# The first pair of a Strassen-style feed-forward layer: the low part of T3 made before the sum T4, and B12 loaded before B21

## The chip, the cores and the metric

One core of one Trainium2 chip runs the whole program in one launch. The metric is the device time in microseconds (us), as the median of the runs of a kernel. Nothing is shared with another core.

## What is computed

Two transformer blocks on 256 tokens of width 1024, batch 1, all in float32. The first block has a forgetting attention beside a multi-scale pooling, an attention over 256 memory tokens, and a gated feed-forward layer. The second has two layers, each of them feed-forward, mixer (a short gated convolution in one, a differential attention in the other), feed-forward. That makes five feed-forward layers, and they are what matters here. Each is

```python
gu = xn @ w_gate_up                                # (256, 1024) @ (1024, 2 * 2816)
act = silu(gu[..., :2816]) * gu[..., 2816:]
h = h + act @ w_down                               # (256, 2816) @ (2816, 1024)
```

(in the second block, what is added is normed and halved first).

## The kernel before

**Precision.** Every float32 weight tile of 128 x 2048 is split into a high part (`w_hi`, made by ScalarE with a copy to the matmul's rounded format, L768 or L1082) and a low part (`w_lo`, made by VectorE as the weight minus its high part, L1359). TensorE then forms each product from three matmuls (L2102 to L2104, and L2558 to L2560 in the down projection): low x times high w, high x times low w, high x times high w. So a tile, called a unit here, passes ScalarE, then VectorE, then TensorE. The high and low buffers are rings of three: ScalarE may write the high part of a unit once TensorE has used the unit three before it.

**The feed-forward layer.** The 2816 gate and up columns go in three plain groups (N0, N1, N2) of 256 and four pairs (p = 0 to 3) of 512. In a pair the gate and the up columns of the two halves of the depth form a 2 x 2 block of weights, B11, B12, B21, B22, and the pair is multiplied in the Strassen-Winograd manner with seven block products P1 to P7 in place of eight. The sums are T1 = B11 + B12, T2 = T1 + B22, T3 = B12 + B22 and T4 = T2 + B21 (the signs lie on the side of x). P1 takes B11, P2 takes B21, P3 takes B22, P4 takes T4, P5 takes T1, P6 takes T2, P7 takes T3. In code a sum is written by VectorE (`weight_sum`, L1378) or by a DMA that adds as it lands (`add_block`, L600: T3 is made in B12's own place from B12 and B22, and T4 of pairs 1 and 2 in T2's place). Places: B11 and B12 are the two halves of the tile `Z`, B21 is `QT`, B22 is `nat`, T1 is `KT`, T2 and then T4 is `VD`, and T3 overwrites B12 in `Z`.

**Order of work.** Each engine runs a list that is written out by hand, and semaphores join the lists. TensorE's order in the first pair is P1, P2, P5, P6, P3, P7, D0, P4, D1, where D0 and D1 are the first two blocks of the down projection (their weights come through `w_raw`). A block product is 12 matmuls, a down block 24. Before each unit TensorE waits for the count of low parts (`w_lo`). D1 also waits for the low part of its own activations (`act_lo`, L1815), which VectorE makes late in the pair. Then comes pair 1: P1, P5, P6, P3, P7, the down block Da, P2, P4, Db.

VectorE's list in the first pair ends: low of P5, P6, P3, the sum T4, low of P7, low of D0, low of P4, result C22 (L1797), low of D1, result C12 (L1799), the sum T1 of pair 1 (L1378, writes `KT`), `act_lo` (L1815), result C11 (L1801). Then the low part of pair 1's P1 follows. ScalarE's list there: high of P3, a copy of P5's product (`keep`, L1113, waits for TensorE's P5), high of P7, a copy of P6's product, high of D0, high of P4 (waits for T4), high of D1, `act_hi` (L1119).

SyncE issues the loads, in order, each behind the wait that its target buffer is free. `next_block(name, reader, p)` loads a block of the next pair once the low part of the product that reads the old one is made. B21 is read in the first pair by P2 and by the sum T4, and so waits for T4 as well:

```python
sp.wait_ge(w_lo, u0 + OP[reader, p] - 1)
if name == "B21" and p == 0:
    sp.wait_ge(t_ok, sums_ready(f, 0, "T4"))
```

VectorE's wait ahead of a low part, and TensorE's ahead of a unit, are these two lines:

```python
dve.wait_ge(w_hi, u - 1)        # lo_of: the high part of this unit is there
pe.wait_ge(w_lo, u - 1)         # block: the low part of this unit is there
```

The functions that the change touches:

Of the kernel before, what the change touches and what calls it, by code (L numbers as in the profile page):

```python
# [135 lines left out]
def raw_slot(u):  # L136

    return LOAD[u] % RING
# [19 lines left out]
def build(nc, a, out):  # L158
# [5 lines left out]
    with ctx:  # L164
# [217 lines left out]
        block = ctx.enter_context(nc.Block())  # L382
# [20 lines left out]
        @block.sync  # L403
        def _(sp):
            def load(u, parts):

                if LOAD[u] >= RING:
                    before = LOADED[LOAD[u] - RING]
                    sp.wait_ge(*((w_lo, before - 1) if before > 1 else (w0_lo, 4 * before + 4)))
                for dst, src in parts:  # L410
                    sp.dma_start(dst, src).then_inc(w_loaded[raw_slot(u)], 16)

            def k_unit(u, w, k0, col):

                v = w.rearrange("(k p) f -> p k f", p=P)
                r = raw[raw_slot(u)][:, :].rearrange("p (k c) -> p k c", k=4)
                load(u, [(r[:, i:i + 2, :], v[:, k0 + i:k0 + i + 2, col:col + HALF]) for i in (0, 2)])

            def block_in(name, p, w_gu):

                gu = w_gu.rearrange("(k p) f -> p k f", p=P)
                k0, col = 4 * (name[1] == "2"), 512 + 512 * p + FF * (name[2] == "2")
                r = WB[name].rearrange("p (k c) -> p k c", k=4)
                for i in (0, 2):
                    sp.dma_start(r[:, i:i + 2, :], gu[:, k0 + i:k0 + i + 2, col:col + HALF]).then_inc(b_in[name], 16)

            def ffn(f, w_gu, w_dn, first_blocks=None, next_gu=None):

                u0 = U_FFN[f]
                gu = w_gu.rearrange("(k p) f -> p k f", p=P)  # L430

                def up(name):
                    u = u0 + OP[name, 0]
                    j = {"N0": 0, "N1": 1, "N2": FJ - 1}[name[:2]]
                    k0 = 4 * (name[-1] == "b")
                    r = raw[raw_slot(u)][:, :].rearrange("p (k c) -> p k c", k=4)
                    load(u, [(r[:, :, 0:256], gu[:, k0:k0 + 4, j * 256:j * 256 + 256]),
                             (r[:, :, 256:512], gu[:, k0:k0 + 4, j * 256 + FF:j * 256 + FF + 256])])

                def down(name, p=0):  # L440
                    u, d = u0 + OP[name, p], down_block(name, p)
                    rows = w_dn[d * 256:d * 256 + 256, :].rearrange("(k p) f -> p k f", p=P)
                    load(u, [(raw[raw_slot(u)][:, D * k:D * k + D], rows[:, k, :]) for k in range(2)])

                def next_block(name, reader, p):

                    if p + 1 < SQUARES or next_gu is not None:
# [3 lines that stand above are left out]
                        block_in(name, (p + 1) % SQUARES, w_gu if p + 1 < SQUARES else next_gu)  # L451

                def first_block(name):
                    if first_blocks:
                        block_in(name, 0, w_gu)

                up("N0a")
                up("N0b")
                up("N1a")
                if f == 4:  # L460
                    for w in first_blocks:
                        sp.wait_ge(*w)
                    first_block("B11")
                up("N1b")
                if f in (0, 2):
                    for w in first_blocks:
                        sp.wait_ge(*w)
                    first_block("B11")
                first_block("B12")
                first_block("B21")  # L470
                first_block("B22")
                down("D0")
                down("D1")
                down("Da", 0)
                next_block("B11", "P1", 0)
                next_block("B22", "P3", 0)
                next_block("B21", "P2", 0)
                next_block("B12", "P7", 0)
                down("Db", 0)
                down("Da", 1)  # L480
                for p in range(1, SQUARES):
                    next_block("B11", "P1", p)
                    next_block("B22", "P3", p)
                    next_block("B12", "P7", p)
                    if p == 1:
                        down("Db", 1)
                        next_block("B21", "P2", p)
                        down("Da", 2)
                    elif p == 2:
                        down("Db", 2)  # L490
                        next_block("B21", "P2", p)
                        up("N2a")
                    else:
                        up("N2b")
                        next_block("B21", "P2", p)
                        down("Da", 3)
                        down("Db", 3)
                        down("DN2")

            def k_groups(u0, w, cols):  # L500
                for g, col in enumerate(cols):
                    k_unit(u0 + 2 * g, w, 0, col)
                    k_unit(u0 + 2 * g + 1, w, 4, col)

            w_in = a["w_in"][0].rearrange("(k p) f -> p k f", p=P)
            for n in range(4):
                if n == 0:
                    sp.dma_start(h[:, 0, :], a["x"][0, 0:P, :]).then_inc(in_x[0], 16)
                c = n % 2 * 2 * HALF
                sp.dma_start(raw[n // 2][:, c:c + 2 * HALF].rearrange("p (k c) -> p k c", k=2),  # L510
                             w_in[:, 2 * n:2 * n + 2, 0:HALF]).then_inc(in_w0[n], 16)
            sp.dma_start(h[:, 1, :], a["x"][0, P:2 * P, :]).then_inc(in_x[1], 16)
            k_unit(U_IN + 2, a["w_in"][0], 0, 512)
            k_unit(U_IN + 3, a["w_in"][0], 4, 512)
            k_groups(U_IN + 4, a["w_in"][0], (1024, 1536))
            k_groups(U_MK, a["w_mem_kv"][0], (0,))
            for n, (k0, col) in enumerate(((4, 0), (4, 512), (0, 0), (0, 512))):
                k_unit(U_OUT + n, a["w_out"][0], k0, col)
            k_unit(U_MV0, a["w_mem_kv"][0], 0, 512)
            k_groups(U_MQ, a["w_mem_q"][0], (0,))  # L520
            k_unit(U_MV1, a["w_mem_kv"][0], 4, 512)
            k_unit(U_MO, a["w_mem_out"][0], 0, 0)
            k_unit(U_MO + 1, a["w_mem_out"][0], 0, 512)
            ffn(0, a["w_gate_up"][0], a["w_down"][0], [(mo_t, 2)], a["ffn_w_gu_2"][0, 0])
            ffn(1, a["ffn_w_gu_2"][0, 0], a["ffn_w_down_2"][0, 0])
            k_groups(U_CIN, a["conv_w_in_2"][0], (0, 1024, 2048, 1536, 2560, 512))
            k_groups(U_COUT, a["conv_w_out_2"][0], (0, 512))
            ffn(2, a["ffn_w_gu_2"][0, 1], a["ffn_w_down_2"][0, 1], [(conv_t, 8), (xt_lo, XT["cout"] + 8)],
                a["ffn_w_gu_2"][1, 0])
            ffn(3, a["ffn_w_gu_2"][1, 0], a["ffn_w_down_2"][1, 0])  # L530
            k_groups(U_K, a["w_kv_2"], (0, 512))
            k_groups(U_Q0, a["attn_w_q_2"][0], (0,))
            k_groups(U_V0, a["w_kv_2"], (1024,))
            k_groups(U_Q1, a["attn_w_q_2"][0], (512,))
            k_groups(U_V1, a["w_kv_2"], (1536,))
            for n, (k0, col) in enumerate(((0, 0), (0, 512), (4, 0), (4, 512))):
                k_unit(U_O + n, a["attn_w_o_2"][0], k0, col)
            ffn(4, a["ffn_w_gu_2"][1, 1], a["ffn_w_down_2"][1, 1], [(ao_t, 4)])
            for t in range(TOKS):
                for half in range(2):  # L540
                    sp.wait_ge(h_up, h_ready("out", t, half))
                    sp.dma_start(out[0, t * P:t * P + P, half * HALF:half * HALF + HALF],
                                 h[:, t, half * HALF:half * HALF + HALF]).then_inc(out_done, 16)
            sp.wait_ge(out_done, 64)
# [802 lines left out]
        def _(dve):  # L1347
# [402 lines left out]
            def ffn(f, stat, reader, gain, update=lambda t: None, kv=False):  # L1750
# [76 lines left out]
                block("P5", 0)  # L1827
                block("P6", 0)
                block("P3", 0)
                weight_sum("T4", f, 0)  # L1830
                block("P7", 0)
                weights("D0")
                block("P4", 0)
                result("C22", 0)
# [1092 lines left out]
```

## Time and profile before

| what | value |
|---|---|
| time, median of 3 runs | 1271.47 us (1270.14 to 1271.62) |
| profiled execution, first to last instruction | 1269.6 us |
| TensorE (PE) busy | 1253.5 us, 99% |
| VectorE (DVE) busy | 1042.7 us, 82% |
| ScalarE (ACT) busy | 804.0 us, 63% |
| GpSimd (POOL) busy | 192.4 us, 15% |
| granted TensorE clock | 0.999 of full speed |

The profile is of one execution, and its span from the first to the last instruction is all that is recorded of that execution's own time. The three timed runs lie 0.5 to 2.0 us above this span. Matmul records overlap: one of 128x512 lasts 0.39 us in a record, but the next starts 0.23 us after it, so starts say more of TensorE's pace than durations do. VectorE's and ScalarE's records overlap a little at their ends too.

### The profile page before, as it was taken

What the parts mean: (1) busy time and instruction counts of PE and PEld (TensorE: products, weight loads), DVE (VectorE), ACT (ScalarE), POOL (GpSimd) and SP (SyncE); (2) the same over time, 40 slices, a digit from 0 to 9 for tenths busy, and PEclk for the clock granted to TensorE, in tenths of its full rate; (3) what the DMA queues carried; (4) which work ended last, traced back from release to release, by engine and by line L of the source; (5) the groups of instructions that cost most, each with busy time, mean ns of one, the idle gap of its engine ahead of it and who ended that gap; (6) DMA issues with size and microseconds to landing.
All of it is one profiled execution on the core that took longest, in us unless ns stands there. A gap on an engine that the chain in (4) does not pass through costs nothing.

```text
span 1269.6 us, 15538 instructions
## 1 busy us (share of the span) xinstructions
PE 1253.5 (99%) x5897; PEld 1028.9 (81%) x5897; DVE 1042.7 (82%) x1035; ACT 804.0 (63%) x986; POOL 192.4 (15%) x224
## 2 busy tenths in 40 slices
PE   9999999999999999999999999999999999999998
PEld 7888878888888878788778888788888877788886
DVE  6766689999799996767899997999977568999984
ACT  6674576665576664645766664766656466766662
POOL 6142130110001100102201101111001003301100
PEclk9999999999999999999999999999999999999999
DMA  9537498997649955568979978389745535999931
GB/s 333 174 100 231 133 313 254 268 270 248 201 151 255 269 168 180 188 226 215 320 249 245 271 251 255 116 237 274 219 166 173 184 125 168 315 286 262 266 135 44
DMA packets 143002, 277.32 MB, mean 218 GB/s; under 512 B 8992, under 2 KB 39896, under 8 KB 142928
## 3 DMA queue, kind: packets, MB, share of 16 engines
q1 hardware_dynamic: 120192, 229.67, 51.6%
q0 software_dynamic: 22288, 45.54, 19.7%
q10 hardware_dynamic: 448, 1.12, 0.2%
q8 instruction: 47, 0.77, 0.2%
q14 instruction: 27, 0.22, 0.1%
HBM read 275.24 MB, written 1.05 MB: 218 GB/s over the span
## 4 chain that ended last, share of the span: by engine, by line
PE 77%; DVE 12%; issue 4%; ACT 3%; DMA 3%; POOL 0%; DVEq 0%; SPq 0%; ACTq 0%
PE B L2102 14%; PE B L2104 14%; PE B L2103 14%; DVE w_lo L1359 7%; PE B L2558 6%; PE B L2560 6%; PE B L2559 6%; PE T L2102 3%; PE T L2104 3%; PE T L2103 3%; DMA VD<-in_ffn_w_gu 2%; DVE VD L1378 1%; DMA Z<-in_ffn_w_gu 1%; ACT w_hi L1082 1%; ACT w_hi L768 1%
## 5 line engine op out<-in xcount | busy, mean ns | idle before, releaser
L1359 DVE TENSOR_TENSOR w_lo<-w_raw,w_hi 128x2048 fp32r<-128x2048 f32 x129 | 296.5, 2299 | 87.5 <-ACT w_hi L768 87.2
L768 ACT ACTIVATE w_hi<-w_raw 128x2048 fp32r<-128x2048 f32 x129 | 247.1, 1918 | 102.7 <-PE B L2560 60.3
L2102 PE MATMUL B<-w_hi,xt_lo 128*128 128x512 f32 x652 | 260.5, 400 | 5.1 <-DVE w_lo L1359 2.1
L2104 PE MATMUL B<-w_hi,xt_hi 128*128 128x512 f32 x652 | 254.7, 391 | 0.0
L2103 PE MATMUL B<-w_lo,xt_hi 128*128 128x512 f32 x652 | 254.0, 390 | 0.0
L2558 PE MATMUL B<-w_hi,act_lo 128*128 128x512 f32 x440 | 172.5, 392 | 0.8 <-DVE w_lo L1359 0.4
L2560 PE MATMUL B<-w_hi,act_hi 128*128 128x512 f32 x440 | 171.4, 390 | 0.0
L2559 PE MATMUL B<-w_lo,act_hi 128*128 128x512 f32 x440 | 171.3, 389 | 0.0
L2102 PEld LDWEIGHTS B<-w_hi,xt_lo 128*128 128x128 f32 x652 | 122.4, 188 | 36.1 <-issue 6.2
L2104 PEld LDWEIGHTS B<-w_hi,xt_hi 128*128 128x128 f32 x652 | 122.4, 188 | 26.4
L2103 PEld LDWEIGHTS B<-w_lo,xt_hi 128*128 128x128 f32 x652 | 122.6, 188 | 23.3
L2102 PE MATMUL B<-w_hi,mem_T_lo 128*128 128x512 f32 x296 | 118.7, 401 | 0.9 <-DVE w_lo L1359 0.9
L2104 PE MATMUL B<-w_hi,mem_T_hi 128*128 128x512 f32 x296 | 115.7, 391 | 0.0
L2103 PE MATMUL B<-w_lo,mem_T_hi 128*128 128x512 f32 x296 | 115.4, 390 | 0.0
L1082 ACT ACTIVATE w_hi<-VD 128x2048 fp32r<-128x2048 f32 x40 | 76.8, 1919 | 55.4 <-PE B L2560 34.8
L2558 PEld LDWEIGHTS B<-w_hi,act_lo 128*128 128x128 f32 x440 | 82.6, 188 | 19.7 <-DVE w_lo L1359 2.0
L2560 PEld LDWEIGHTS B<-w_hi,act_hi 128*128 128x128 f32 x440 | 82.5, 188 | 17.4
L2559 PEld LDWEIGHTS B<-w_lo,act_hi 128*128 128x128 f32 x440 | 82.6, 188 | 16.6
L1359 DVE TENSOR_TENSOR w_lo<-Z,w_hi 128x2048 fp32r<-128x2048 f32 x40 | 91.4, 2286 | 4.6 <-ACT w_hi L1082 4.6
L1359 DVE TENSOR_TENSOR w_lo<-VD,w_hi 128x2048 fp32r<-128x2048 f32 x40 | 91.5, 2287 | 3.0 <-ACT w_hi L1082 3.0
L600 POOL DMA_DIRECT2D Z<-in_ffn_w_gu x32 | 39.0, 1449 | 338.4 <-DVE KT L1378 338.4
L1082 ACT ACTIVATE w_hi<-Z 128x2048 fp32r<-128x2048 f32 x40 | 76.5, 1913 | 9.1 <-PE B L2104 5.1
(330 smaller groups left out, 2110.0 us busy)
## 6 DMA issues: line engine op xcount, KB each, us to landing
w_raw<-in_ffn_w_down SPq DMA_DIRECT2D x88, 512.0 KB, 5.8
Z<-in_ffn_w_gu SPq DMA_DIRECT2D x64, 512.0 KB, 8.1
w_raw<-in_ffn_w_gu SPq DMA_DIRECT2D x48, 512.0 KB, 5.2
nat<-in_ffn_w_gu SPq DMA_DIRECT2D x32, 512.0 KB, 7.8
QT<-in_ffn_w_gu SPq DMA_DIRECT2D x32, 512.0 KB, 7.0
Z<-in_ffn_w_gu POOLq DMA_DIRECT2D x32, 512.0 KB, 8.8
w_raw<-in_conv_w_in SPq DMA_DIRECT2D x24, 512.0 KB, 4.7
w_raw<-in_w_down SPq DMA_DIRECT2D x22, 512.0 KB, 6.6
```

Of the source, the lines that this page charges most:

```text
L600: pool.dma_start(r[:, i:i + 2, :], gu[:, 4 + i:6 + i, col:col + HALF], accum_op=ALU.add)\
L768: act.activation(whi[home(u)][:, :], raw[slot][:, :], ACT.Copy).then_inc(w_hi, 1)
L1082: act.activation(whi[home(u)][:, :], (WB[src] if src in WB else WT[src]), ACT.Copy).then_inc(w_hi, 1)
L1359: dve.tensor_tensor(wlo[home(u)][:, :], src, whi[home(u)][:, :].bitcast(F32), ALU.subtract).then_inc(w_lo, 1)
L1378: dve.tensor_tensor(WT[name], src, WB[block_name], ALU.add).then_inc(t_ok, 1)
L2102: pe.matmul(bank[:, :], lo[:, k, x], whi[s][:, c], start=first, stop=False, skip_group_check=more)
L2103: pe.matmul(bank[:, :], hi[:, k, x], wlo[s][:, c], start=False, stop=False, skip_group_check=more)
L2104: return pe.matmul(bank[:, :], hi[:, k, x], whi[s][:, c], start=False, stop=last, skip_group_check=more)
L2558: pe.matmul(o, lo[:, x], whi[slot][:, c], start=d == 0 and k == 0, stop=False)
L2559: pe.matmul(o, hi[:, x], wlo[slot][:, c], start=False, stop=False)
L2560: ins = pe.matmul(o, hi[:, x], whi[slot][:, c], start=False, stop=d == FJ - 1 and k == 1)
```

## The change

Two neighbouring lines change places in each of two lists. VectorE makes the low part of P7's operand (T3) ahead of the sum T4. SyncE issues the load of pair 1's B12 (which waits for that low part) ahead of the load of B21 (which waits for T4). It applies once in each of the five feed-forward layers.

```diff
@@ SyncE, ffn()
                 next_block("B11", "P1", 0)
                 next_block("B22", "P3", 0)
+                next_block("B12", "P7", 0)
                 next_block("B21", "P2", 0)
-                next_block("B12", "P7", 0)
                 down("Db", 0)
                 down("Da", 1)
@@ VectorE, ffn()
                 block("P3", 0)
+                block("P7", 0)
                 weight_sum("T4", f, 0)
-                block("P7", 0)
                 weights("D0")
                 block("P4", 0)
                 result("C22", 0)
```

On VectorE, in the first pair of a feed-forward layer (`VD<-VD,QT` is the sum T4; the low parts read `nat` for P3, `Z` for P7, `w_raw` for D0 and `VD` for P4):

```order
 L1359 TENSOR_TENSOR w_lo<-VD,w_hi 128x2048
 L1359 TENSOR_TENSOR w_lo<-nat,w_hi 128x2048
-L1378 TENSOR_TENSOR VD<-VD,QT 128x2048
-L1359 TENSOR_TENSOR w_lo<-Z,w_hi 128x2048
+L1359 TENSOR_TENSOR w_lo<-Z,w_hi 128x2048
+L1378 TENSOR_TENSOR VD<-VD,QT 128x2048
 L1359 TENSOR_TENSOR w_lo<-w_raw,w_hi 128x2048
 L1359 TENSOR_TENSOR w_lo<-VD,w_hi 128x2048
```

The sum and P7's low part have changed places; both stay ahead of D0's low part.

On SyncE's queue, at the same place (`nat` is B22 of pair 1, `Z` B12, `QT` B21; the `w_raw` loads behind them are for Db and Da):

```order
 L425 DMA Z<-in_ffn_w_gu 128x2x512 x2
 L425 DMA nat<-in_ffn_w_gu 128x2x512 x2
+L425 DMA Z<-in_ffn_w_gu 128x2x512 x2
 L425 DMA QT<-in_ffn_w_gu 128x2x512 x2
-L425 DMA Z<-in_ffn_w_gu 128x2x512 x2
 L411 DMA w_raw<-in_ffn_w_down 128x1024 x4
```

B12's two transfers now stand in front of B21's two. TensorE's, ScalarE's and GpSimd's lists are the same in both kernels.

## Rows read from the trace of the kernel before

**Rows 1.** The page: the span, and busy time of each engine.

```profile
span 1269.6 us, 15538 instructions
...
PE 1253.5 (99%) x5897; PEld 1028.9 (81%) x5897; DVE 1042.7 (82%) x1035; ACT 804.0 (63%) x986; POOL 192.4 (15%) x224
```

**Rows 2.** Who PE waited for: us in total, times, longest.

```profile
PE T L2102 <- DVE w_lo L1359: 1.2, 5, 0.2
```

**Rows 3.** Timeline of PE, first layer: start, us, line, operation, [idle before <-releaser].

```profile
202.08 0.39 PE L2104 MATMUL B<-w_hi,mem_T_hi 128*128 128x512 f32 x1
202.71 0.47 PE L2102 MATMUL T<-w_hi,mem_T_lo 128*128 128x512 f32 x1 [0.24 <-DVE w_lo L1359]
203.02 0.40 PE L2103 MATMUL T<-w_lo,mem_T_hi 128*128 128x512 f32 x1
203.25 0.39 PE L2104 MATMUL T<-w_hi,mem_T_hi 128*128 128x512 f32 x1
...
205.53 0.39 PE L2558 MATMUL B<-w_hi,act_lo 128*128 128x512 f32 x1
...
210.97 0.39 PE L2102 MATMUL T<-w_hi,xt_lo 128*128 128x512 f32 x1
...
213.70 0.40 PE L2558 MATMUL B<-w_hi,act_lo 128*128 128x512 f32 x1
...
224.59 0.39 PE L2102 MATMUL B<-w_hi,mem_T_lo 128*128 128x512 f32 x1
```

**Rows 4.** Timeline of DVE in the same stretch.

```profile
198.07 2.29 DVE L1378 TENSOR_TENSOR VD<-VD,QT 128x2048 f32<-128x2048 f32 x1
200.28 2.29 DVE L1359 TENSOR_TENSOR w_lo<-Z,w_hi 128x2048 fp32r<-128x2048 f32 x1
202.48 2.29 DVE L1359 TENSOR_TENSOR w_lo<-w_raw,w_hi 128x2048 fp32r<-128x2048 f32 x1
204.68 2.29 DVE L1359 TENSOR_TENSOR w_lo<-VD,w_hi 128x2048 fp32r<-128x2048 f32 x1
206.88 0.68 DVE L1797 TENSOR_TENSOR work<-work,T 128x512 f32<-128x512 f32 x1
207.74 2.29 DVE L1359 TENSOR_TENSOR w_lo<-w_raw,w_hi 128x2048 fp32r<-128x2048 f32 x1 [0.17 <-ACT w_hi L768]
209.95 0.68 DVE L1799 TENSOR_TENSOR work<-B,work 128x512 f32<-128x512 f32 x1
210.55 2.28 DVE L1378 TENSOR_TENSOR KT<-Z 128x2048 f32<-128x2048 f32 x1
212.75 0.68 DVE L1815 TENSOR_TENSOR act_lo<-T,act_hi 128x512 fp32r<-128x512 f32 x1
...
221.88 2.28 DVE L1359 TENSOR_TENSOR w_lo<-VD,w_hi 128x2048 fp32r<-128x2048 f32 x1
```

**Rows 5.** Timeline of ACT in the same stretch.

```profile
197.06 0.60 ACT L1113 ACTIVATE work<-B 128x512 f32<-128x512 f32 x1 [1.23 <-PE B L2104]
197.56 1.91 ACT L1082 ACTIVATE w_hi<-Z 128x2048 fp32r<-128x2048 f32 x1
...
200.28 1.91 ACT L768 ACTIVATE w_hi<-w_raw 128x2048 fp32r<-128x2048 f32 x1
202.56 1.92 ACT L1082 ACTIVATE w_hi<-VD 128x2048 fp32r<-128x2048 f32 x1 [0.37 <-PE B L2104]
205.79 1.92 ACT L768 ACTIVATE w_hi<-w_raw 128x2048 fp32r<-128x2048 f32 x1 [1.30 <-PE T L2104]
...
211.23 0.60 ACT L1119 ACTIVATE act_hi<-T 128x512 fp32r<-128x512 f32 x1 [3.52 <-PE B L2560]
```

**Rows 6.** Timeline of DVE, then of PE, third layer: T1, and D1's first matmul.

```profile
660.72 2.29 DVE L1378 TENSOR_TENSOR KT<-Z 128x2048 f32<-128x2048 f32 x1 [0.46 <-DMA Z<-in_ffn_w_gu]
...
663.09 0.39 PE L2104 MATMUL T<-w_hi,xt_hi 128*128 128x512 f32 x1
663.76 0.47 PE L2558 MATMUL B<-w_hi,act_lo 128*128 128x512 f32 x1 [0.28 <-DVE act_lo L1815]
```

**Rows 7.** DMA issues by tile: count, KB each, us from issue to landing.

```profile
QT<-in_ffn_w_gu SPq DMA_DIRECT2D x32, 512.0 KB, 7.0
```

## The prediction

> **What bounds the kernel now.** I read the page first: TensorE is busy for 1253.5 of 1269.6 us, VectorE for 82% and ScalarE for 63% [rows 1]. So a change can win only what TensorE waits, and loses whatever it makes TensorE wait. Next, the table of waits, for TensorE: one of its rows is a wait for a low part ahead of matmuls into bank T, five times, 1.2 us together [rows 2]. There are five feed-forward layers, and the timeline shows that this is P7's first matmul: it starts 0.63 us after the last one of P3, where neighbours are 0.23 us apart [rows 3]. The full price is read from starts: from 202.08 to the second matmul of P7 at 203.02 is 0.94 us, against 2 x 0.227 = 0.45 undisturbed, so 0.49 us a layer (0.08 of it because the matmul behind a wait is followed after 0.31 us, not 0.23).
>
> Why it waits stands in VectorE's timeline: T4 at 198.07, P7's low part at 200.28, which ends at 202.57, and P7 starts 0.14 us later [rows 3, 4]. VectorE's big operations are issued 2.20 us apart and last 2.29. So the sum T4 stands in front of something that TensorE needs sooner. That is what the change takes away. The same stretch then has to be followed to the end, since VectorE goes on without a gap from here to D1.
>
> **Edit 1, P7's low part ahead of T4.** VectorE is free at 198.07. But the low part needs the high part, and ScalarE writes that from 197.56 to 199.47 [rows 5]. It can't be earlier: ahead of it ScalarE copies P5's product, and that copy at 197.06 waited 1.23 us for TensorE. VectorE follows ScalarE within 0.03 us: the high part of D1 ends at 205.79 + 1.92 = 207.71 and its low part starts at 207.74 [rows 4, 5]. So in the new order P7's low part starts at 199.50, and **VectorE stands idle for 1.43 us** where T4 ran before. Everything behind is in order on VectorE:
>
> - P7's low part: 199.50 to 201.78. TensorE can start at 201.92, and wants P7 at 202.08 + 0.23 = 202.31. No wait; 0.49 us won.
> - T4: 201.70 to 203.99 (before 198.07 to 200.36).
> - D0's low part: 203.90 to 206.19 (before 202.48 to 204.77). Its high part is there at 202.19 [rows 5].
> - P4's low part: its high part now waits for T4, and runs from 204.02 to 205.94 (before from 202.56). VectorE takes it at 206.10.
>
> Now D0. TensorE would reach it at 205.53 - 0.49 = 205.04 [rows 3]. Its low part is there at 206.19 + 0.14 = 206.33. With the 0.08 us behind a wait, TensorE is at 206.41 where it was at 205.53: **the 0.49 us won at P7 become a loss of 0.88 us at D0.** Before, D0 had 205.53 - 204.77 - 0.14 = 0.62 us to spare; the idle of 1.43 us eats that and the gain.
>
> Then D1, which waits for `act_lo`. VectorE: C22 at 208.30, D1's low part at 208.90 (high part: 205.84 to 207.76, so the old wait of 0.17 us is gone), C12 at 211.10, T1 at 211.70, `act_lo` from 213.90 to 214.58; the intervals are those of rows 4. Its `act_hi` is behind the end of D0 (211.23 before, about 212.1 now [rows 5]) and is not last. TensorE reaches D1 at 206.41 + 24 + 12 matmuls (5.44 + 2.73 from the starts 205.53, 210.97, 213.70 [rows 3]) = 214.58. `act_lo` lets it go at 214.58 + 0.14 = 214.72, and 0.08 follows: 214.80 against 213.70, **a loss of 1.10 us**.
>
> What is late next: VectorE is now 1.15 us behind its old times, TensorE 1.10. In pair 1 the closest meeting is P6: its low part ends at 221.88 + 2.28 = 224.16 and its first matmul was at 224.59 [rows 3, 4], 0.29 us to spare after the 0.14; of this 0.05 us goes. From there ScalarE and VectorE follow TensorE's own progress, and all run 1.10 us late in step. Nothing returns the loss later in the layer, as TensorE is the bound.
>
> The third layer differs. There T1 waited 0.46 us for B12, so D1 already started at 663.76 where 663.09 + 0.23 = 663.32 was possible [rows 6]: it lost 0.52 us with the 0.08. All of the first layer's times hold there with 449.65 us added, so the new D1 stands at 214.80 + 449.65 = 664.45 against 663.84 with its 0.08: a loss of 0.61 us.
>
> **Edit 2, B12 ahead of B21.** B12 is issued when P7's low part is done, 201.9 in place of 202.6, and T1 that reads it starts 1.15 us later than before: so the wait of 0.46 us in the third layer vanishes (counted above), elsewhere it costs nothing. Had B21 stayed in front, B12 would have waited for T4 as well, until 204.0, and with the same time to land T1 would wait in more layers; the second edit avoids this. B21 goes out at 204.1 in place of 200.4 and needs 7.0 us [rows 7]. It is read by P2 of pair 1, which TensorE reaches after D1, five block products and a down block, 5.4 + 5 x 2.7 + 5.4 = 24 us after 213.7. Without that cover the load would cost its 3.7 us; with it nothing. Of the two steps behind it on SyncE, the load for Db goes from the end of D0's low part as before, 1.4 us later, for a unit used in pair 1's last step.
>
> **The sum.** 4 x 1.10 + 0.61 = 5.0 us. Against the profiled span of 1269.6 that is 1274.6; the median of the runs is 1271.47, 1.9 us above that span, and what lies around the span doesn't change: **1276.5 us**, 0.4% slower.
>
> *Bounds of the unknown.* The order of before shows no wait at D0, so its price is worked out, not read. From below: if D1's `act_lo` comes in time (it misses by 0.14 us only), each layer loses 0.88 and the third 0.88 - 0.52 = 0.36: 3.9 us. From above: if P6 of pair 1 is late too, the whole idle of 1.43 reaches TensorE with 0.08 behind it: 1.51 a layer, 1.0 in the third, 7.0 us. I take the value between by the rows, since each margin is read to about 0.05 us.
>
> On VectorE's pace the trace differs from a rule. The rows have the next operation start 0.08 us ahead of the end of the one before [rows 4]. The Trainium skill, VectorE: DVE Perf Modes, section "The DRAIN you can't avoid", says that the next operation does not start until the pipe is empty. Read as the end of the record, that would put 0.08 us more on each queued operation, two of them between P7's low part and D0's: 0.16 us a layer, 0.8 us in all, 1277.3. The rows show the shorter step, so they set the sum.
>
> **The rivals.**
>
> *Only the gap at P7 counts* (ends on the other side). If VectorE's idle did not exist, or D0's low part were still in time, the change would win 0.49 us a layer, 2.45 us: 1269.0. For it: the gap is real and D0 has slack. It needs the idle on VectorE to be 0.54 us or less (0.62 to spare less 0.08: then TensorE is at D0 where it was), and wholly none at D0 below 0.13 us. ScalarE's row says 1.43. It would also come about if VectorE ran the sum while the low part waits, that is if the change did not do what its order says; no row shows VectorE passing a waiting operation. 7 in 100. The Trainium skill, Perfetto Trace Analysis, section "Optimization Strategy", says to find the gaps on the most contended engine and make what ends them start sooner; by that rule alone this rival is the forecast, and its time is the same 1269.0. The trace agrees that there is such a gap; by the rows it is handed on to a place 3 us behind it.
>
> *The loss is caught up.* If TensorE's delay only uses up waits that it has later in the layer for things that don't move (a load, an addition by DMA), half of it could return: 2.5 us, 1274.0. Against it: TensorE's waits that I found are for VectorE's low parts and `act_lo`, whose chain moves along. 5 in 100.
>
> *The delay grows along pair 1.* If VectorE loses another 0.3 us, say because the gates behind C11 come late, P6 waits as well and a second wait costs its 0.08: about 1.6 us a layer, 8 us: 1279.5. For it: margins of 0.24 us. Against: ScalarE has room there. 8 in 100.
>
> **The numbers.** The forecast, a loss of 3.9 to 7.0 us, has 80 in 100. A measurement of this kernel tells about 0.2%, 2.5 us, from no change. Faster by more: only the first rival with luck, 3. Within: the rest of it and the second rival, 9. Slower: 88. The range reaches from 1274.3 (the lower bound's 1275.4 less 1.1 us, since the three runs lie 1.5 us apart) to 1278.8 (just over the upper bound's 1278.5).
>
> **What the new profile would show.** P7's row without its wait for a low part; VectorE idle about 1.4 us ahead of the low part from `Z`, released by ScalarE's high part; a new wait of about 1.2 us at D0 (first matmul of L2558) for the low part from `w_raw`, five times; a small one at D1 for `act_lo`, five times; none for T1 on the load of B12 in the third layer's first pair. I am wrong if VectorE starts P7's low part before 199, or if D0's first matmul comes less than 0.5 us behind the end of P7.

## The result

The changed kernel takes 1276.09 us (median of 4 runs, 1275.65 to 1276.81) against 1270.81 us before (4 runs, one more than in the table above, 1269.42 to 1271.62): ratio 1.0046, 95% interval 1.0033 to 1.0058, or 4.2 to 7.4 us slower. Measured again later beside the other experiments it was 1.0047 (1.0035 to 1.0060). The profiled execution spans 1274.2 us, 4.6 us more than the one of before.

The page after: span and busy time.

```profile
span 1274.2 us, 15538 instructions
...
PE 1254.1 (98%) x5897; PEld 1028.6 (81%) x5897; DVE 1042.6 (82%) x1035; ACT 803.6 (63%) x986; POOL 192.2 (15%) x224
```

TensorE's busy time is what it was but for 0.6 us [rows 1]; the added time is idle time. The table of waits for TensorE (us in total, times, longest) says where. One of its rows, before and then after:

```profile
PE B L2558 <- DVE w_lo L1359: 0.4, 1, 0.4
```

```profile
PE B L2558 <- DVE w_lo L1359: 5.3, 5, 1.1
```

The row of P7's matmuls into bank T [rows 2] is no longer in the table. In its place L2558, the down projection, waits for a low part five times, 5.3 us together, each time at D0. (The one wait of before was at Db of pair 2 in the second layer, and isn't among the five after.) The timeline of TensorE in the first layer, after, as in [rows 3] (this execution reached P3 of the first layer 0.32 us sooner than the one of before, so times are compared from the last matmul of P3, 202.08 before and 201.76 here):

```profile
201.76 0.39 PE L2104 MATMUL B<-w_hi,mem_T_hi 128*128 128x512 f32 x1
201.99 0.39 PE L2102 MATMUL T<-w_hi,mem_T_lo 128*128 128x512 f32 x1
...
205.94 0.50 PE L2558 MATMUL B<-w_hi,act_lo 128*128 128x512 f32 x1 [1.06 <-DVE w_lo L1359]
206.27 0.40 PE L2559 MATMUL B<-w_lo,act_hi 128*128 128x512 f32 x1
...
214.02 0.39 PE L2104 MATMUL T<-w_hi,xt_hi 128*128 128x512 f32 x1
214.43 0.47 PE L2558 MATMUL B<-w_hi,act_lo 128*128 128x512 f32 x1
214.74 0.39 PE L2559 MATMUL B<-w_lo,act_hi 128*128 128x512 f32 x1
```

P7 starts 0.23 us after P3, without a wait. D0 starts 4.18 us after P3's last matmul, 3.45 before: 0.73 late, and 0.83 with the 0.10 that the next matmul (0.33 behind it) adds. D1 starts 12.67 us after it, 11.62 before: 1.05 late, and 1.13 with its own 0.08. The 0.41 us from 214.02 to 214.43, where 0.23 is the step, is the wait for `act_lo`: too short to stand as idle time, since records overlap.

VectorE in the same stretch, as in [rows 4], and then ScalarE's high part of P7 as in [rows 5]:

```profile
195.55 2.29 DVE L1359 TENSOR_TENSOR w_lo<-nat,w_hi 128x2048 fp32r<-128x2048 f32 x1
199.19 2.29 DVE L1359 TENSOR_TENSOR w_lo<-Z,w_hi 128x2048 fp32r<-128x2048 f32 x1 [1.34 <-ACT w_hi L1082]
201.40 2.28 DVE L1378 TENSOR_TENSOR VD<-VD,QT 128x2048 f32<-128x2048 f32 x1
203.60 2.29 DVE L1359 TENSOR_TENSOR w_lo<-w_raw,w_hi 128x2048 fp32r<-128x2048 f32 x1
...
213.60 0.69 DVE L1815 TENSOR_TENSOR act_lo<-T,act_hi 128x512 fp32r<-128x512 f32 x1
...
197.24 1.91 ACT L1082 ACTIVATE w_hi<-Z 128x2048 fp32r<-128x2048 f32 x1
```

VectorE could have started at 195.55 + 2.20 = 197.75 and starts at 199.19, 0.04 after ScalarE's high part ends at 197.24 + 1.91 = 199.15. The 1.44 us are the idle time; the record says 1.34, because it counts from the end of the record before. T4 and D0's low part then follow at 2.20.

The third layer, after: T1 on VectorE, and TensorE's last matmul of P3 and first of D1, as in [rows 6].

```profile
663.20 2.29 DVE L1378 TENSOR_TENSOR KT<-Z 128x2048 f32<-128x2048 f32 x1
...
653.57 0.39 PE L2104 MATMUL B<-w_hi,mem_T_hi 128*128 128x512 f32 x1
666.24 0.47 PE L2558 MATMUL B<-w_hi,act_lo 128*128 128x512 f32 x1
```

T1 no longer waits for B12. D1 comes 12.67 us after P3, as in the first layer; before it was 663.76 - (202.08 + 449.65) = 12.03, so this layer loses 0.64 us.

### The profile page after: what moved, and what is told of

It reads as the page before. It is cut to its first block, busy times and chain, and to the rows that moved or that the text cites. A ratio compares the mean times of both kernels' runs of the same rounds, so it can differ in the third digit from the quotient of the medians.

```text
span 1274.2 us, 15538 instructions
## 1 busy us (share of the span) xinstructions
PE 1254.1 (98%) x5897; PEld 1028.6 (81%) x5897; DVE 1042.6 (82%) x1035; ACT 803.6 (63%) x986; POOL 192.2 (15%) x224
## 3 DMA queue, kind: packets, MB, share of 16 engines
HBM read 275.24 MB, written 1.05 MB: 217 GB/s over the span
## 4 chain that ended last, share of the span: by engine, by line
PE 77%; DVE 12%; ACT 4%; issue 3%; DMA 3%; POOL 0%; DVEq 0%; SPq 0%; ACTq 0%
PE B L2102 14%; PE B L2104 14%; PE B L2103 14%; PE B L2558 7%; DVE w_lo L1359 7%; PE B L2560 7%; PE B L2559 6%; PE T L2102 3%; PE T L2104 3%; PE T L2103 3%; DMA VD<-in_ffn_w_gu 2%; DVE VD L1378 1%; PE T L2582 1%; ACT w_hi L1082 1%; ACT w_hi L768 1%
## 5 line engine op out<-in xcount | busy, mean ns | idle before, releaser
L2558 PE MATMUL B<-w_hi,act_lo 128*128 128x512 f32 x440 | 173.5, 394 | 5.4 <-DVE w_lo L1359 5.3
L2558 PEld LDWEIGHTS B<-w_hi,act_lo 128*128 128x128 f32 x440 | 82.6, 188 | 26.8 <-DVE w_lo L1359 8.2
```

Source lines behind the costliest of these rows:

```text
L2558: pe.matmul(o, lo[:, x], whi[slot][:, c], start=d == 0 and k == 0, stop=False)
```

## The experiments

Two theories were to be told apart. Mine: VectorE idles until ScalarE has made P7's high part, and T4, which used to fill that time, then stands in front of D0's low part and of `act_lo`. The first rival: the new order of the loads does it. The second: the idle as such, or anything at all behind P7's low part, does it. Times are medians, with that of before from the same set of runs; ratios have their 95% interval.

**Only the sum's order.** The changed kernel with SyncE's old order:

```diff
+                next_block("B21", "P2", 0)
                 next_block("B12", "P7", 0)
-                next_block("B21", "P2", 0)
```

> VectorE's half of the change alone: P7's low part ahead of T4, but B21 loaded ahead of B12 as before. Theory (VectorE idles 1.4 us for ScalarE's high part of P7, so D0 and D1 are late): D0 loses 0.8 to 0.9 us a layer as with the whole change, and since B12 now waits on SyncE's queue behind B21, which waits for T4, T1 and with it D1 get later still: 1276 if B12 lands in 6 us, 1284 if it takes 9; most likely 1281. Rival (the new order of the loads causes the loss): no loss here, 1270.8 or less.

1278.69 against 1271.28 us, 1.0053 (1.0041 to 1.0066), 5.2 to 8.4 us slower. The loss is there without the new order of the loads, as my theory says, but it is less than the most likely number, 1281: B12 landed sooner than I had assumed for it. VectorE's T1, then TensorE's D0 and D1, in the first layer:

```profile
212.02 2.29 DVE L1378 TENSOR_TENSOR KT<-Z 128x2048 f32<-128x2048 f32 x1 [0.52 <-DMA Z<-in_w_gate_up]
...
205.95 0.50 PE L2558 MATMUL B<-w_hi,act_lo 128*128 128x512 f32 x1 [1.06 <-DVE w_lo L1359]
215.06 0.47 PE L2558 MATMUL B<-w_hi,act_lo 128*128 128x512 f32 x1 [0.61 <-DVE act_lo L1815]
```

D0 has the same wait of 1.06 us; D1's has grown to 0.61 as T1 waits 0.52 for B12. Counted from P3, D1 comes 0.1 to 0.6 us later than with both edits, 1.4 us over the five layers. So by this trace (of the fastest of the five runs) the second edit is worth 1.4 us beside the first; by the times alone that isn't shown, since the intervals of this run and of the whole change overlap.

**Only the loads' order.** The kernel before with SyncE's new order:

```diff
+                next_block("B12", "P7", 0)
                 next_block("B21", "P2", 0)
-                next_block("B12", "P7", 0)
```

> SyncE's half of the change alone: B12 loaded ahead of B21, T4 ahead of P7's low part as before. Theory: P7 keeps its wait of 0.49 us, D0 has no wait; B12 lands a little sooner, which can win up to 0.5 us in the third layer: 1270.3 to 1270.8. Rival (the loads cause the loss): 1275 to 1276.

1271.90 against 1271.28, 1.0003 (0.9994 to 1.0012): no difference. The first rival falls. The gain of up to 0.5 us that I expected can't be seen in the times. In the trace its cause is there: T1 in the third layer starts without the wait of 0.46 us that it had before [rows 6], and D1 there is 0.5 us sooner:

```profile
661.36 2.28 DVE L1378 TENSOR_TENSOR KT<-Z 128x2048 f32<-128x2048 f32 x1
```

**T4 cut to 8 columns.** The changed kernel; the sum leaves out 2040 of T4's 2048 columns, so the result is not that of the layer. (The added wait is for P6's low part, which reads the tile that the sum overwrites; VectorE made it three operations earlier.)

```diff
+                cut = 8 if name == "T4" and p == 0 else UNIT
+                if cut == 8:
+                    dve.wait_ge(w_lo, U_FFN[f] + OP["P6", 0] - 1)
-                dve.tensor_tensor(WT[name], src, WB[block_name], ALU.add).then_inc(t_ok, 1)
+                dve.tensor_tensor(WT[name][:, 0:cut], src[:, 0:cut], WB[block_name][:, 0:cut], ALU.add).then_inc(t_ok, 1)
```

> The changed order, but T4 of the first pair is formed on 8 of its 2048 columns only, so P4's product leaves out most of B21. Theory: VectorE still idles 1.4 us ahead of P7's low part, but T4's 2.2 us no longer stand in front of D0's low part, which is in time: P7's 0.49 us are won in all five layers, and 0.5 us at D1 in the third: 1267.8. Rival (the idle itself, or the later P7 on VectorE, costs the time, not the sum behind it): 1273 to 1276.

1268.56 against 1271.28, 0.9975 (0.9966 to 0.9984), 2.0 to 4.3 us faster. VectorE, then TensorE's D0:

```profile
200.03 2.29 DVE L1359 TENSOR_TENSOR w_lo<-Z,w_hi 128x2048 fp32r<-128x2048 f32 x1 [1.34 <-ACT w_hi L1082]
202.23 0.16 DVE L1381 TENSOR_TENSOR VD<-VD,QT 128x8 f32<-128x8 f32 x1
...
205.32 0.39 PE L2107 MATMUL T<-w_hi,mem_T_hi 128*128 128x512 f32 x1
205.55 0.39 PE L2561 MATMUL B<-w_hi,act_lo 128*128 128x512 f32 x1
```

VectorE idles the same 1.34 us, and TensorE loses nothing: D0 follows P7 after 0.23. So the idle by itself is free where the sum's 2.2 us don't follow it. It is the two together that are dear. The second rival falls in its first half.

**T4 in two pieces, 1280 columns ahead of P7's low part.**

```diff
-                block("P7", 0)
-                weight_sum("T4", f, 0)
+                half = weight_sum("T4", f, 0, 0)
+                block("P7", 0)
+                dve.wait_ge(dve_step, half)
+                weight_sum("T4", f, 0, 1)
```

The last argument names the piece: 0 is columns 0 to `FIRST` (1280 here), 1 the rest. The edit inside `weight_sum` that cuts the columns isn't shown.

> The changed order, but T4 is cut in two: 1280 columns ahead of P7's low part, where VectorE idles, 768 behind it. Theory: the first piece takes 1.40 of the 1.43 us of idle, the second 0.87 us; D0's low part is there at 205.0 in the first layer's time, just when TensorE wants it. P7 wins 0.49 us a layer, D1 still waits for act_lo and loses 0.26: 0.23 us a layer, 0.75 in the third, 1.7 in all: 1269.1. Rival (any T4 work behind P7's low part makes D0 late): 1273 or more.

1270.07 against 1271.28, 0.9990 (0.9981 to 0.9999), 0.1 to 2.4 us faster. VectorE, then TensorE's D0 and D1 in the first layer, each with the matmul ahead of it:

```profile
198.59 1.49 DVE L1382 TENSOR_TENSOR VD<-VD,QT 128x1280 f32<-128x1280 f32 x1
200.00 2.28 DVE L1360 TENSOR_TENSOR w_lo<-Z,w_hi 128x2048 fp32r<-128x2048 f32 x1
202.20 0.95 DVE L1382 TENSOR_TENSOR VD<-VD,QT 128x768 f32<-128x768 f32 x1
...
205.28 0.39 PE L2115 MATMUL T<-w_hi,mem_T_hi 128*128 128x512 f32 x1
205.51 0.39 PE L2569 MATMUL B<-w_hi,act_lo 128*128 128x512 f32 x1
...
213.47 0.39 PE L2115 MATMUL T<-w_hi,xt_hi 128*128 128x512 f32 x1
213.90 0.47 PE L2569 MATMUL B<-w_hi,act_lo 128*128 128x512 f32 x1
```

The first piece takes 1.41 us from start to start and fits the idle. Work of T4 still stands behind P7's low part, but D0 isn't late (0.23 us behind the matmul ahead): the second rival falls altogether. D1 still waits for `act_lo`, 0.43 us behind the matmul ahead, and gives back 0.28 of the 0.49 us won at P7; 0.26 was expected.

**The same, cut at 640** (`FIRST = 640`).

> T4 cut at 640: 640 columns ahead of P7's low part, 1408 behind it. Theory (the loss is what of T4 doesn't fit into the idle): 0.70 us of idle are left, the second piece takes 1.53 us, D0's low part is 0.62 us late for a TensorE without its wait at P7: D0 loses 0.2 us a layer, D1 0.43, the third layer gains 0.1: 1.6 us slower, 1272.4. Rival (splitting as such removes the loss, wherever the cut is): as with the cut at 1280.

1272.85 against 1271.43, 1.0010 (1.0001 to 1.0019), 0.1 to 2.4 us slower. The second piece of T4 and D0's low part on VectorE, then D0, in the first layer:

```profile
201.65 1.62 DVE L1382 TENSOR_TENSOR VD<-VD,QT 128x1408 f32<-128x1408 f32 x1
203.18 2.29 DVE L1360 TENSOR_TENSOR w_lo<-w_raw,w_hi 128x2048 fp32r<-128x2048 f32 x1
...
205.52 0.50 PE L2569 MATMUL B<-w_hi,act_lo 128*128 128x512 f32 x1 [0.40 <-DVE w_lo L1360]
```

The wait is 0.40 us, between 1.06 (nothing of T4 in the idle) and none (1280 columns in it). The second piece takes 1.53 us from start to start where the whole sum took 2.20, 0.67 less, and 1.06 less 0.67 is 0.39: the wait goes with what of T4 stands behind P7's low part.

**P7's high part first on ScalarE.** The changed kernel with

```diff
                 block("P3", 0)
-                keep("P5", 0)
                 block("P7", 0)
+                keep("P5", 0)
                 keep("P6", 0)
```

> The whole change, and ScalarE makes P7's high part ahead of the copy of P5's product, 0.5 us sooner. Theory: VectorE's idle shrinks from 1.4 to 0.9 us, D0 loses 0.4 us in place of 0.85 and D1 0.6 in place of 1.1: 2.5 us slower than before in all, 1273.3, somewhat more if P3 waits for the copy. Rival (the idle is not what makes D0 late): as with the change, 1276.

1275.16 against 1271.43, 1.0026 (1.0015 to 1.0037), 1.9 to 4.7 us slower. VectorE's P7, then TensorE's first two matmuls of P3, and D0:

```profile
199.46 2.29 DVE L1359 TENSOR_TENSOR w_lo<-Z,w_hi 128x2048 fp32r<-128x2048 f32 x1 [0.88 <-ACT w_hi L1082]
...
199.97 0.49 PE L2102 MATMUL B<-w_hi,mem_T_lo 128*128 128x512 f32 x1
200.30 0.39 PE L2103 MATMUL B<-w_lo,mem_T_hi 128*128 128x512 f32 x1
206.21 0.50 PE L2558 MATMUL B<-w_hi,act_lo 128*128 128x512 f32 x1 [0.50 <-DVE w_lo L1359]
```

The idle went from 1.34 to 0.88 and D0's wait from 1.06 to 0.50. P3 now pays 0.10 us (0.33 between its first two matmuls) and starts 0.06 us after the end of the copy of P5's product, which now comes late. The time lies between my number and the rival's, and its interval meets that of the whole change (from 1.0033), so it is the trace that decides: with a smaller idle D0 waits less.

**C12 behind `act_lo`, with the whole change.** T1 and `act_lo` come 0.6 us sooner:

```diff
-                result("C12", 0)
                 weight_sum("T1", f, 1)
                 act_out(1)
+                result("C12", 0)
                 result("C11", 0)
```

> The whole change, and C12 behind act_lo on VectorE. Theory: the loss has two terms, 0.82 us at D0 and another 0.3 at D1 for act_lo; made 0.6 us sooner, act_lo is in time and only D0's term is left: 3.6 us slower than before, 1275. Rival (D1's wait is not a term of its own): as the change, 5 us slower.

1275.68 against 1271.42, 1.0040 (1.0027 to 1.0054), 3.4 to 6.9 us slower; the changed kernel beside it:

> The changed kernel again, to have it beside the others on the same chip: 5.0 us slower than before, by all theories.

1277.05, 1.0047 (1.0035 to 1.0060). The times differ by 1.4 us as expected, but their intervals overlap, so the trace has to decide. D0, and D1 with the matmul ahead of it, with C12 late:

```profile
206.72 0.50 PE L2558 MATMUL B<-w_hi,act_lo 128*128 128x512 f32 x1 [1.06 <-DVE w_lo L1359]
...
214.80 0.39 PE L2104 MATMUL T<-w_hi,xt_hi 128*128 128x512 f32 x1
215.03 0.39 PE L2558 MATMUL B<-w_hi,act_lo 128*128 128x512 f32 x1
```

D0's wait is untouched and D1's is gone (0.23 us from the matmul ahead): two terms, as predicted. Not all of D1's 0.28 us is won: P6 of pair 1, which had 0.24 us to spare by the prediction's count, now pays 0.11 in the same trace, so a layer gains 0.17.

**Both: T4 cut at 1280 and C12 late.**

> T4 cut at 1280, and C12 behind act_lo on VectorE, so that T1 and act_lo are made 0.6 us sooner, T1 still ahead of act_lo. Theory: P7, D0 and D1 all start without a wait in the four layers alike, 0.49 us each, and the third wins 0.5 us more: 3.0 us faster than the kernel before, 0.2%, 1268.4, if T1 doesn't have to wait for B12. Rival (T1 now waits for B12 to land): as the cut alone, 1.3 us faster.

1269.55 against 1271.42, 0.9986 (0.9977 to 0.9995), 0.6 to 2.9 us faster, less than the 3.0 that I expected. TensorE at P6 of pair 1 (last matmul of P5, then the first two of P6):

```profile
223.42 0.39 PE L2115 MATMUL B<-w_hi,mem_T_hi 128*128 128x512 f32 x1
223.69 0.47 PE L2113 MATMUL B<-w_hi,mem_T_lo 128*128 128x512 f32 x1
224.00 0.40 PE L2114 MATMUL B<-w_lo,mem_T_hi 128*128 128x512 f32 x1
```

P7, D0 and D1 have no wait left. P6 of pair 1 has one now: 0.58 us for two steps, 0.12 more than undisturbed. That explains some 0.6 us over five layers; the rest is within the interval. By the times this kernel can't be told from the one with the cut alone (0.9990).

**`act_lo` ahead of T1** was the mistake. Tried with the cut at 1280 and alone on the kernel before:

```diff
                 result("C12", 0)
-                weight_sum("T1", f, 1)
-                act_out(1)
                 result("C11", 0)
+                act_out(1)
+                weight_sum("T1", f, 1)
```

> T4 cut at 1280 as before, and act_lo of D1 (with C11) ahead of T1 on VectorE. Theory: D1's wait for act_lo is gone too, in all layers: 0.49 us a layer and 1.0 in the third, 3.0 in all: 1267.8, if the later T1 (2.3 us or so later than in the kernel before) still lets the addition to T3 land before pair 1's P7. Rival (T1 is needed that early): P7 of pair 1 waits, and the time is 1270 or more.

> The kernel before, with act_lo of D1 (and C11) ahead of T1 on VectorE and nothing else. Theory: only the third layer had a wait there, 0.5 us: 1270.3. Rival: the later T1 delays pair 1, 1271 to 1273.

1280.97 and 1282.34 against 1271.43: 1.0072 (1.0059 to 1.0084) and 1.0086 (1.0073 to 1.0098), 7.5 to 12.5 us slower. My theory's number was wrong in both. The rivals named with them have the place right, pair 1, but not the size: the second one's rival said 1271 to 1273. The first layer: GpSimd's addition to T3 and ScalarE's high part of P4 in pair 1, in the kernel before; then, in the second of the two kernels, VectorE's T1, GpSimd's addition, ScalarE's high parts of P7 and of P4 in pair 1, and TensorE's P6 and Db of pair 1:

```profile
213.13 2.37 POOL L600 DMA_DIRECT2D Z<-in_w_gate_up  x2 [31.18 <-DVE KT L1378]
...
234.62 1.92 ACT L1082 ACTIVATE w_hi<-VD 128x2048 fp32r<-128x2048 f32 x1 [1.49 <-DMA VD<-in_w_gate_up]
```

```profile
212.18 2.28 DVE L1378 TENSOR_TENSOR KT<-Z 128x2048 f32<-128x2048 f32 x1
214.76 2.37 POOL L600 DMA_DIRECT2D Z<-in_w_gate_up  x2 [33.16 <-DVE KT L1378]
...
226.36 1.92 ACT L1082 ACTIVATE w_hi<-Z 128x2048 fp32r<-128x2048 f32 x1 [1.22 <-DMA Z<-in_w_gate_up]
236.47 1.92 ACT L1082 ACTIVATE w_hi<-VD 128x2048 fp32r<-128x2048 f32 x1 [3.09 <-DMA VD<-in_w_gate_up]
...
224.75 0.47 PE L2102 MATMUL B<-w_hi,mem_T_lo 128*128 128x512 f32 x1 [0.30 <-DVE w_lo L1359]
245.76 0.50 PE L2558 MATMUL B<-w_hi,act_lo 128*128 128x512 f32 x1 [0.69 <-DVE w_lo L1359]
```

T1 also releases GpSimd's addition to T3. With T1 1.63 us later that addition goes out 1.63 us later (213.13 and 214.76), and ScalarE waits 1.22 us for it where it didn't wait before. ScalarE's wait for the addition to T4 grows from 1.49 to 3.09 us. That addition is released by P6's low part and goes out only 0.44 us later; why it lands later still was not tested. TensorE pays at P6, and most at Db, 30 us after the place that was changed. I had followed TensorE's wait and not the DMA that T1 sets off.

## Why the prediction was right

- *The gap at P7, 0.49 us a layer, goes.* Shown: P7 follows P3 after 0.23 us.
- *VectorE idles 1.43 us.* 1.44 in the trace, released by ScalarE's high part 0.04 us before. With a smaller idle (P7's high part first) or with work in it (the cuts at 640 and 1280) the loss shrinks in step.
- *D0 turns the gain into a loss of 0.88 us.* 0.83 measured: TensorE went 0.07 us sooner than I had it (0.05 us after the end of the low part, where I took the 0.14 of P7), and the restart costs 0.10, not 0.08.
- *D1 adds to it, 1.10 in all; the third layer 0.61.* 1.13 and 0.64. Four times 1.13 and 0.64 is 5.2 us (forecast 5.0), against 5.3 between the medians. The span grew by 4.6: that execution was 0.32 us quicker to its first pair, and in the third layer before, TensorE lost another 0.3 us at Db of pair 1, which it doesn't lose after.
- *The second edit costs nothing, and saves T1 a wait.* Alone it does nothing to the time (1.0003), though T1's wait in the third layer goes; without it T1 waits 0.52 us in the first layer. The median without it was 2.6 us over that of the change, but the intervals of the two ratios overlap.
- *VectorE's pace.* 2.20 to 2.21 us from start to start, 0.08 ahead of the record's end, holds in the new order too, so the reading of the Trainium skill (VectorE: DVE Perf Modes, "The DRAIN you can't avoid") that would have added 0.8 us is not borne out; the section itself makes an exception of a next operation that isn't held.
- *The rivals.* That only the gap counts became true where the sum shrank (0.9975). The growth along pair 1 did not come: P6 had no wait. The loss was not caught up to the half that the second rival names: counted from the first layer's P3 the two traces end 4.9 us apart (4.6 + 0.32), not 5.2. Whether the 0.3 at Db came back through the delay or by chance, as loads land at different times from run to run, was not tested.

What the prediction left out: that the idle can be filled with part of the sum, so that P7's wait goes and D0 isn't late. The better order is neither of the two: T4 in two pieces, C12 late, 0.9986 (0.9977 to 0.9995).

## What to carry to other kernels

An operation that stands in front of something urgent may stand there because the urgent thing can't start anyway: before moving it, read when the urgent one's own input is ready, and count the time between as idle on that engine. On an engine that works in order, everything behind is then later by that idle time, here 1.44 us at D0's low part, and the next urgent item pays what is left of it after its slack. Work that fills such a gap should be cut to its size; and before moving anything, follow every engine and DMA that its semaphore releases, not only the one that is seen to wait.

## What the runs showed of the hardware that was not expected

A matmul that had to wait costs more than its wait: the next one comes 0.31 to 0.34 us after it in place of 0.23 (205.94 to 206.27 at D0, 214.43 to 214.74 at D1). The prediction had 0.31 from P7; the 0.33 at D0 is new. TensorE also starts sooner behind the low part of a down block: 0.05 us after its record ends (203.60 + 2.29 = 205.89, and 205.94), against 0.14 at P7 before (202.57 and 202.71) and at D1 (214.29 and 214.43). The reason was not tested. And the landing of loads differs between executions of one kernel. T1's waits for B12 over the whole program (us in total, times, longest), in the changed kernel and in the same kernel run again:

```profile
DVE KT L1378 <- DMA Z<-in_ffn_w_gu: 0.2, 1, 0.2
```

```profile
DVE KT L1378 <- DMA Z<-in_ffn_w_gu: 1.7, 3, 0.8
```

Their spans are 1274.2 and 1275.5 us. These waits explain little of that: 0.81 of the 1.3 us lie ahead of the first layer's last matmul of P3 (201.76 and 202.57). So one trace of this kernel is sure to about 1 us only, though the starts of D0 and D1, counted from P3, repeat to 0.01 in all five layers; why the loads land differently was not tested.
